# SBUF areas of a decoder-trunk kernel placed at multiples of 128 bytes, with three 32-byte tiles moved behind the work area

## The reference, cut to what matters

```python
for layer in range(DEPTH):                       # 2
    h = rmsnorm(x, mix_norm_g[layer])
    x = x + hybrid_mixer(h, w_in[layer], ..., w_out[layer])
    h = rmsnorm(x, ffn_norm_g[layer])
    if layer % 2 == 0:
        x = x + swiglu(h, dense_w_gate[i], dense_w_up[i], dense_w_down[i])   # 1024 x 2816
    else:
        x = x + moe_swiglu(h, router_w[i], moe_w_gate[i], moe_w_up[i], moe_w_down[i])  # 8 x 1024 x 3584
return rmsnorm(x, final_norm_g)

def swiglu(h, wg, wu, wd):
    return (jax.nn.silu(h @ wg) * (h @ wu)) @ wd
```

## Time and profile before

| | |
|---|---|
| median of 3 runs | 1518.66 us (1517.97 to 1518.70) |
| span of the profiled execution | 1515.6 us |
| between this span and the median, outside the first and last instruction | 3.1 us |
| TensorE busy with matmuls | 1476.9 us (97%) |
| VectorE busy | 1171.2 us (77%) |
| ScalarE busy | 978.1 us (65%) |
| moved by DMA | 426.53 MB, mean 281 GB/s |
| granted TensorE clock, mean | 0.994 |

### The profile page before, as it was taken

One profiled execution on the slowest core, in us unless ns is written; L12 is line 12 of the kernel. 1 busy time (PEld: TensorE's weight loads), 2 busy tenths in 40 slices (PEclk: granted clock), 3 DMA queues, 4 the chain that ended last, 5 costly groups with the idle time before them and its releaser, 6 DMA issues.

```text
span 1515.6 us, 21913 instructions
## 1 busy us (share of the span) xinstructions
PE 1476.9 (97%) x7705; PEld 1245.1 (82%) x7705; DVE 1171.2 (77%) x1295; ACT 978.1 (65%) x1179; POOL 7.3 (0%) x22
## 2 busy tenths in 40 slices
PE   6999999989998999999999999999999999999996
PEld 6888999979987888888888888888888888888885
DVE  5855644548566888988988888888888888888886
ACT  5565433435465776767677767677776776776774
POOL 0000000000000000000000000000000000000000
PEclk9999999999999999999999999999999999999999
DMA  8723755534267999999999999989999999998950
GB/s 305 253 84 98 238 179 191 170 117 176 84 222 253 346 354 363 318 354 369 337 335 354 351 322 358 362 313 355 367 339 330 358 345 330 354 364 312 354 212 28
DMA packets 180493, 426.53 MB, mean 281 GB/s; under 512 B 9200, under 2 KB 31824, under 8 KB 164704
## 3 DMA queue, kind: packets, MB, share of 16 engines
q1 hardware_dynamic: 179664, 423.27, 78.3%
q0 software_dynamic: 784, 2.65, 0.6%
HBM read 424.85 MB, written 1.05 MB: 281 GB/s over the span
## 4 chain that ended last, share of the span: by engine, by line
PE 94%; ACT 2%; DVE 2%; SPq 1%; DMA 1%; issue 0%; DVEq 0%
PE psum L314 29%; PE psum L316 28%; PE psum L315 28%; PE psum L319 6%; PE psum L1549 2%; DMA raw<-in_w_in 1%; PE psum L1215 1%; SPq L346 0%; PE psum L1454 0%; ACT xn L465 0%; DVE soft L945 0%; DVE w_lo L779 0%; ACT rest L579 0%; ACT rest L578 0%; ACT rest L577 0%
## 5 line engine op out<-in xcount | busy, mean ns | idle before, releaser
L1159 DVE TENSOR_TENSOR w_lo<-raw,w_hi 128x1024 fp32r<-128x1024 f32 x666 | 768.7, 1221 | 39.9 <-ACT w_hi L725 39.8
L725 ACT CAST w_hi<-raw 128x1024 fp32r<-128x1024 f32 x666 | 656.5, 1054 | 71.0 <-PE psum L316 69.2
L314 PE MATMUL psum<-w_hi,g_hT 128*128 128x512 f32 x896 | 359.7, 402 | 0.0
L315 PE MATMUL psum<-w_hi,g_hT 128*128 128x512 f32 x896 | 355.3, 397 | 0.0
L316 PE MATMUL psum<-w_lo,g_hT 128*128 128x512 f32 x896 | 355.0, 396 | 0.0
L316 PEld LDWEIGHTS psum<-w_lo,g_hT 128*128 128x128 f32 x896 | 168.5, 188 | 40.9
L314 PEld LDWEIGHTS psum<-w_hi,g_hT 128*128 128x128 f32 x896 | 169.4, 189 | 38.7
L315 PEld LDWEIGHTS psum<-w_hi,g_hT 128*128 128x128 f32 x896 | 168.9, 189 | 38.5
L779 DVE TENSOR_TENSOR w_lo<-raw,w_hi 128x1024 fp32r<-128x1024 f32 x136 | 161.3, 1221 | 45.5 <-ACT w_hi L460 45.0
L460 ACT CAST w_hi<-raw 128x1024 fp32r<-128x1024 f32 x136 | 137.9, 1051 | 70.4 <-PE psum L316 61.6
L314 PE MATMUL psum<-w_hi,aT 128*128 128x512 f32 x448 | 178.4, 398 | 1.5 <-DVE aT L989 1.5
(11 more groups left out here) (211 smaller groups left out, 1642.9 us busy)
## 6 DMA issues: line engine op xcount, KB each, us to landing
raw<-in_moe_w_up SPq DMA_DIRECT2D x112, 1024.0 KB, 7.5
raw<-in_moe_w_down SPq DMA_DIRECT2D x112, 1024.0 KB, 6.6
raw<-in_moe_w_gate SPq DMA_DIRECT2D x112, 1024.0 KB, 6.7
raw<-in_w_in SPq DMA_DIRECT2D x24, 1024.0 KB, 7.3
raw<-in_dense_w_gate SPq DMA_DIRECT2D x11, 1024.0 KB, 5.4
raw<-in_dense_w_up SPq DMA_DIRECT2D x11, 1024.0 KB, 5.3
raw<-in_dense_w_down SPq DMA_DIRECT2D x11, 1024.0 KB, 4.8
raw<-in_w_out SPq DMA_DIRECT2D x8, 1024.0 KB, 5.7
```

The source lines that it names most:

```text
L314: nc.tensor.matmul(ps, a_hi, b_hi, start=start, stop=False, skip_group_check=True)
L315: nc.tensor.matmul(ps, a_lo, b_hi, start=False, stop=False, skip_group_check=True)
L725: a.copy(w_hi[q % RING][:], piece_src(n)).then_inc(hi_done, 1)
L1159: v.tensor_tensor(w_lo[q % RING][:], piece_src(n), w_hi[q % RING][:].bitcast(F32), ALU.subtract).then_inc(split, 1)
```

## The change

`BASE` and every `area` are rounded to 128 instead of 32 bytes. `stat`, `rstd` and `plan` no longer come from `area`: they lie in the last 96 bytes of the usable SBUF, and the work area ends in front of them. The rounding inside `Region` stays at 32 bytes. No instruction is added, removed or reordered.

```diff
 BLOCK = 2 * PIECE
+LINE = 128
...
-        BASE = (nc.sbuf_base + 31) // 32 * 32
+        BASE = (nc.sbuf_base + LINE - 1) // LINE * LINE
         cursor = [BASE]
 
         def area(size):
             at = cursor[0]
-            cursor[0] += (size + 31) // 32 * 32
+            cursor[0] += (size + LINE - 1) // LINE * LINE
             assert cursor[0] <= nc.sbuf_usable_end, (cursor[0], nc.sbuf_usable_end)
             return at
...
-        stat = at("stat", [P, 8], area(32))
-        rstd = at("rstd", [P, 8], area(32))
-        plan = at("plan", [P, 1 + MORE], area(32), I32)
         work_at = cursor[0]
-        WORK = nc.sbuf_usable_end // 32 * 32 - work_at
+        assert work_at % LINE == 0
+        small_at = nc.sbuf_usable_end // 32 * 32 - 3 * 32
+        stat = at("stat", [P, 8], small_at)
+        rstd = at("rstd", [P, 8], small_at + 32)
+        plan = at("plan", [P, 1 + MORE], small_at + 64, I32)
+        WORK = small_at - work_at
         mixer = Region(work_at, WORK)
```

## The result

The changed kernel takes **1490.47 us** (median of 4 runs, 1489.96 to 1491.04) beside 1518.32 us for the kernel before, measured together with it (4 runs, 1517.57 to 1518.70). The ratio is 0.9818, with a 95% interval of 0.9806 to 0.983: 27.9 us less. Forecast were 1491.5 us in a range of 1483 to 1503. The profiled execution took 1491.04 us; its span, from the first to the last instruction, is 1489.3 us.

A forecast was written before the change was run, and what follows sets the result against it. TensorE was taken to bound the kernel through the distance between matmul starts. Terms of -32.2, +3 and +2.0 us gave -27 us, so 1518.66 us became about 1491.5 us, range 1483 to 1503.

The forecast's parts named there:

- What bounds the kernel: Whole kernel: TensorE, busy 97% of the span; time is the number of matmuls times the distance between their starts.
- The 512-column term: Dense part and expert items: 4296 matmuls against work-area tiles step at 226.6 instead of 234.1 ns, 32.2 us off.
- 3 given back: After each of 91 interruptions the 512-column steps need a few matmuls to settle, costing about 3 us.
- Its reason: 512-column matmuls: steps settle when the stationary tile starts at a multiple of 128 bytes, not 96 bytes over one.
- "no change" rival: Whole kernel: SBUF region may decide instead of alignment, or transfers cap the experts; 1518.7 us, chance 0.12.
- The rule of 16-byte lines: Skill text counting SBUF in 16-byte lines: both starts fit, so the sum would be 0, time 1518.7 us; small chance.
- The 256-column term: Dense part: 1056 matmuls against dense_hT go to 120 ns steps, 2.0 us more.
- Its lower end: Dense part's 256-column matmuls: at best a gain in proportion to the 512-column one, 4.0 us less.
- ScalarE, VectorE, small tiles: Work on moved tiles keeps its durations and is hidden, 0; stat, rstd and plan 0, within 0.3 us.
- Does the time stay: Expert items shrink to 123.9 us; VectorE, ScalarE and transfers at 356 GB/s fit, so the gain stands.
- The sum: Whole kernel: -32.2 + 3 + 2.0 = -27 us on a span of 1515.6 us.
- The 3.1 us between span and median: Whole kernel: the median lies 3.1 us above the span, so 27 us were taken off 1518.66 us.

The follow-up runs named there:

- e1: Changed kernel, but the three small tiles stay in front and the work area starts at the next multiple of 128 up: 1514.02 us.
- e4: Changed kernel with BASE raised by 32 bytes, so every area moves and only the three small tiles stay: 1488.96 us.
- e2: Changed kernel with the work area 64 bytes further up, small tiles in the free places in front and behind: 1510.30 us.
- e3: Changed kernel with the work area 32 bytes further up, small tiles in the free places in front and behind: 1513.99 us.
- e7: Changed kernel with the weight rings 32 bytes further up and the areas behind them 256 bytes up: 1514.52 us.
- e8: Changed kernel with the weight rings 96 bytes further up and the areas behind them 256 bytes up: 1517.07 us.
- e9: Changed kernel with dense_hT alone 64 bytes further up: 1487.79 us, ratio 0.9803 to the kernel before.

## Why the prediction was right, and where its reason was wrong

*What bounds the kernel.* Right: the same instructions, the same chain, and only the distance of matmul starts changed.

*The 512-column term.* Right in size. 32.2 us less 3 given back were forecast, of which all but the dense part's share falls on the items, from 127.4 to 123.9 us. Measured are 123.92 us, and 27.9 us over all experts. The dense part kept its length although its 256-column steps took about 2.1 us more (1056 x 2.0 ns), so its 512-column steps gave as much: 30.0 us together, against 29.2. Settling takes the six or so steps that were read from the earlier trace rows.

*Its reason.* **Wrong.** "What settles is `mixer_hT`, at a multiple of 128; what does not is `dense_aT`, `g_hT` and `aT`, 96 bytes over one" took the place of one tile for the cause. The rows supported it only because the moving tile never changed its place in them. e1 (a multiple of 128, 233.2 ns) and e4 (no multiple, 227.2 ns) refute it; the condition is a difference of 0 modulo 256 between stationary and moving start. The change meets it because moving `work_at` down to the next multiple of 128 happened to give 128 over a multiple of 256, as the rings have. The next multiple up, which e1 takes, brought 4.8 us instead of 28. So that the number was met is in part luck: of the two kinds of multiples of 128, 128 over and 0 over a multiple of 256, only the first gives it here, and nothing in the forecast chose between them. The forecast had no chance for that, and should have had one.

*Region.* The part of the "no change" rival which blamed the region is refuted: e2 and e3 lie 64 and 32 bytes beside the changed kernel and step at 233.2 and 233.0 ns instead of 226.7, and in e7 and e8 `mixer_hT` loses its 226.7 ns without moving.

*The rule of 16-byte lines* (the Trainium skill, SBUF — State Buffer, section Specifications (TRN2)) does not tell these cases apart: every start here is a multiple of 16, and the times differ by 28 us. The measurement decides.

*The 256-column term.* Right in sign and size: 117.4 and 118.7 went to 120.0 ns, and the dense part's 512-column gain and this loss cancel, 204.0 us both times. Its lower end, a gain in proportion to 4.0 us, was not low enough for what other differences give (113.3 ns, about 5 us).

*ScalarE, VectorE, small tiles.* Right at 0: busy times agree to 1.4 us, and e1, which leaves the small tiles in front, reaches the dense part after 140.6 us, as the changed kernel does after 140.5. *Does the time stay.* Right: TensorE is busy for all 123.92 us of an item; the DMA rate is 355 GB/s, as worked out.

*Not forecast:* 1.6 us in mixer 1 from the lower clock. The sum, 27 us off the span, met 26.3 between the two profiled executions; without the clock it would have been 27.9. The medians lie 27.9 us apart.

*Readings of rows that were off.* The 3.1 us between span and median are not all time outside the first and last instruction: in the changed kernel, and in every later run of the kernel before, that is 1.7 to 1.8 us (1518.77 and 1517.0, for one). The rest is that the profiled execution of the kernel before was shorter than the median. As the forecast took 27 us off the median, this does not touch its sum. Lines 319, 1549 and 1215 make up 9% of the chain, not 8%. And 119 instructions name `stat`, `rstd` or `plan` in the trace, more than a few dozen; no run puts a price on them.

## What to carry to other kernels

When matmuls follow each other closely, look at the distance of their starts for one shape against different operands; a few per cent between them at the same clock can be a matter of placement. Then vary the place of *both* operands: an observation with one of them fixed cannot tell "aligned" from "aligned to the other". Here equal starts modulo 256 bytes were best for 512 moving columns and among the worst for 256, so one rule for all areas leaves time behind, and a rounding to 128 meets the condition only by luck. What goes before a run counts too: a step measured in one kernel (113.3 ns in e2) was not reached in another at the same difference (117.8 in e9).

## What the runs showed of the hardware that was not expected

Matmuls of one shape, each with its own weight load, have steady step times that go with (stationary start minus moving start) modulo 256: 226.7 to 234.3 ns at 512 columns, 113.3 to 120.0 ns at 256. The sign matters (64: 233.3 ns, 192: 228.9 ns at 512 columns). For 256 columns two steady patterns exist for the same matmuls, 113.3 and 117.8 ns at differences of 64 and 192, and 117.3 and 118.7 ns at 96, depending on what ran before. What in TensorE or SBUF makes them was not found out; differences that are not multiples of 32 were not tried, nor other data types.
